# A fp32-accurate two-block kernel on one core: the places of the modulation steps, the order of the start, and four smaller orders are changed

## The reference, cut to what matters

```python
def first_block(x, c, ...):                 # D = 1024
    cond = silu(c)
    for l in range(2):
        sh1, sc1, g1, sh2, sc2, g2 = split(cond @ w_ada[l] + b_ada[l], 6)   # w_ada[l]: 1024 x 6144
        h = layer_norm(x) * (1 + sc1) + sh1
        mix = mixer(h, ...)                 # w_in, global + dilated attention, gates, w_pa, w_pb, w_out
        x = layer_norm(ALPHA * x + g1 * mix, ln1_g[l], ln1_b[l])
        h = layer_norm(x) * (1 + sc2) + sh2
        ffn = moe(h, ...)                   # router: best group of 4 experts, top 2 of 16, then gate/up/down
        x = layer_norm(ALPHA * x + g2 * ffn, ln2_g[l], ln2_b[l])
    return x

def second_block(x, mem, ...):              # two layers: h = rms_norm(x); retention, pooling, neighbourhood
    ...                                     # attention, attention to mem; gates, w_branch, w_out; then a ffn
```

## Time and profile before

| | before |
|---|---|
| time, median of 3 executions | 1797.58 us (1797.54 to 1797.79) |
| the profiled execution's own time | 1800.65 us |
| its span | 1798.80 us |
| mean granted TensorE clock | 0.976 |
| instructions | 27507 |
| the chain that ended last, by engine | PE 74%, DVE 9%, ACT 5%, POOL 5%, issue 5% |
| HBM read | 390.46 MB, 218 GB/s over the span |
| 1 MB weight transfer, issue to landing | 5.1 to 5.9 us median by name |

### The profile page before, as it was taken

The page is one execution under the profiler, slowest core; times in us unless marked ns, Lnnn a source line. Parts: engine busy times, 40 slices in busy tenths (PEclk is TensorE's granted clock), DMA queues, the critical chain, the costliest instruction groups (busy, mean ns, idle before and its releaser), DMA issues.

```text
span 1798.8 us, 27507 instructions
## 1 busy us (share of the span) xinstructions
PE 1709.0 (95%) x11564; PEld 1506.1 (84%) x11564; DVE 1171.6 (65%) x1288; ACT 939.8 (52%) x1057; POOL 224.6 (12%) x209
## 2 busy tenths in 40 slices
PE   4999997999889999799989999999999999999999
PEld 2888885888678888588869889899999989989998
DVE  2537658899864766889987475565446756665443
ACT  4435535877543554678756454354445545354442
POOL 0330010000024001001004400200001610210000
PEclk9999998999989999899989999999999999999999
DMA  9985566999848525499956445466655644546552
GB/s 363 320 275 181 176 212 235 363 373 374 289 146 282 175 101 190 181 382 376 358 178 222 120 138 165 141 211 211 207 184 184 188 130 129 188 141 209 186 186 76
DMA packets 207306, 393.28 MB, mean 219 GB/s; under 512 B 6129, under 2 KB 143345, under 8 KB 191313
## 3 DMA queue, kind: packets, MB, share of 16 engines
q1 hardware_dynamic: 204768, 381.71, 61.3%
q0 software_dynamic: 1712, 7.50, 1.2%
q10 hardware_dynamic: 704, 2.33, 0.4%
HBM read 390.46 MB, written 1.05 MB: 218 GB/s over the span
## 4 chain that ended last, share of the span: by engine, by line
PE 74%; DVE 9%; ACT 5%; POOL 5%; issue 5%; DMA 1%; SPq 0%; POOLq 0%; DVEq 0%; ACTq 0%
PE ps L546 21%; PE ps L548 21%; PE ps L547 21%; DVE low L1916 3%; PE ps L644 2%; ACT whi L1326 2%; POOL TB L2799 1%; PE ps L847 1%; PE ps L815 1%; DMA AR<-in_w_ada 1%; PE ps L830 1%; PE ps L663 1%; PE ps L564 1%; DVE small L1978 1%; POOL T L2692 1%
## 5 line engine op out<-in xcount | busy, mean ns | idle before, releaser
L1916 DVE TENSOR_TENSOR low<-raw,whi 128x2048 fp32r<-128x2048 f32 x310 | 714.6, 2315 | 393.5 <-ACT whi L1326 391.8
L1326 ACT ACTIVATE whi<-raw 128x2048 fp32r<-128x2048 f32 x310 | 591.4, 1913 | 335.3 <-PE ps L548 305.5
L546 PE MATMUL ps<-Hh,whi 128*128 128x256 f32 x1536 | 438.8, 286 | 0.0
L547 PE MATMUL ps<-Hl,whi 128*128 128x256 f32 x1536 | 434.4, 283 | 0.0
L548 PE MATMUL ps<-Hh,low 128*128 128x256 f32 x1536 | 434.4, 283 | 0.0
L546 PE MATMUL ps<-whi,Hh 128*128 128x256 f32 (+1 forms) x896 | 294.4, 329 | 27.1 <-DVE T L1964 9.9
L546 PEld LDWEIGHTS ps<-Hh,whi 128*128 128x128 f32 x1536 | 294.3, 192 | 17.4 <-issue 16.9
L547 PEld LDWEIGHTS ps<-Hl,whi 128*128 128x128 f32 x1536 | 294.4, 192 | 0.5
L548 PEld LDWEIGHTS ps<-Hh,low 128*128 128x128 f32 x1536 | 294.4, 192 | 0.0
L547 PE MATMUL ps<-low,Hh 128*128 128x256 f32 (+1 forms) x896 | 289.7, 323 | 0.0
L548 PE MATMUL ps<-whi,Hl 128*128 128x256 f32 (+1 forms) x896 | 289.4, 323 | 0.0
(11 more groups left out here) (325 smaller groups left out, 2161.5 us busy)
## 6 DMA issues: line engine op xcount, KB each, us to landing
raw<-in_w_gu SPq DMA_DIRECT2D x80, 1024.0 KB, 5.6
raw<-in_w_ff SPq DMA_DIRECT2D x66, 1024.0 KB, 5.1
raw<-in_w_in SPq DMA_DIRECT2D x58, 1024.0 KB, 5.9
raw<-in_w_d SPq DMA_DIRECT2D x40, 1024.0 KB, 5.7
raw<-in_w_gate SPq DMA_DIRECT2D x32, 1024.0 KB, 5.4
ada<-in_w_ada SPq DMA_DIRECT2D x18, 1024.0 KB, 7.1
G<-in_w_ada SPq DMA_DIRECT2D x16, 1024.0 KB, 8.4
raw<-in_w_out SPq DMA_DIRECT2D x16, 1024.0 KB, 5.0
```

Source lines behind the costliest of these rows:

```text
L546: pe.matmul(out, lhs[0], rhs[0], start=start, stop=False)
L547: pe.matmul(out, lhs[0], rhs[1], start=False, stop=False)
L1326: act.activation(wide(i, whi), wide(i, raw), ACT.Copy).then_inc(*up("w_hi", i))
L1916: dve.tensor_tensor(wide(i, low), wide(i, raw), wide(i, whi).bitcast(F32), ALU.subtract).then_inc(*up("w_lo", i))
```

## The change

It does this:

- Start: PE lifts only tile 0 ahead of steps 4 to 7 and sums 2 and 3, and tile 1 behind them; the second "qa" bank is taken when tile 1 begins. ACT makes hi 0, lift 0, hi 1 to 3, then issues the transfer of `rows`, then lift 1. DVE makes lo 0 within lift 0, then lo 1 to 3, then lift 1.
- Modulation: a new place "x1" stands between the transposes of the router's two tiles. Layer 0 takes steps 31 to 33 at x1, 34 and 35 at rt, 36 to 41 at the end of its moe ("ff"); layer 1 takes 42 at vd2, 43 at qk1, 44 to 46 at x1 and 47 at rt. Sums 15 (rt), 16 and 17 (moe) and 18 (ff) are made in layer 0, 19 (vd1), 20 (vd2), 21 (qk2), 22 (rt) and 23 (moe) in layer 1. Slots, rows and SP's order of transfers follow; two slots lie over the buffer B. ACT's turn "rt" stands right behind the sigmoid, ACT's mod_out 18 and 19 ahead of the first norm of layer 1.
- End of layer 1's moe: put_back(0) and put_back(1) stand ahead of mem_lift(0) on PE, and ACT and DVE split the unit for the last down product ahead of it.
- Second block, layer 0: DVE lifts tile 0 after tile 1's first half of the residual; PE lifts it between mk and mv of the second memory tile; ACT makes the norm of tile 1 after the copy of mv.
- ACT's copies of the turned rq and rk each stand one place sooner, in both layers.
- The second block's `out_proj` lifts tile 0 ahead of part i == 3.

```diff
@@ -214,11 @@
 MOD_PLACES = ["qa", "vd1", "vd2"] + [f"qk{i}" for i in range(6)] + [f"at{i}" for i in range(10)] + ["pa", "out", "xT", "rt"]
-MOD_TAKEN = [{"qa": (8, 9)} | {place: (10 + i,) for i, place in enumerate(MOD_PLACES[1:])},
-             {"qa": (35,)} | {place: (36 + i,) for i, place in enumerate(MOD_PLACES[1:13])}]
-MOD_SUMMED = [{"vd2": 4, "pa": 13, "xT": 14, "moe": 15} | {f"qk{i}": 5 + i // 2 for i in (1, 3, 5)} | {f"at{i}": 8 + i // 2 for i in (1, 3, 5, 7, 9)},
-              {"vd1": 16, "vd2": 17} | {f"qk{i}": 18 + i // 2 for i in (1, 3, 5)} | {f"at{i}": 21 + i // 2 for i in (1, 3, 5)}]
+MOD_TAKEN = [{"qa": (8, 9)} | {place: (10 + i,) for i, place in enumerate(MOD_PLACES[1:22])}
+             | {"x1": (31, 32, 33), "rt": (34, 35), "ff": (36, 37, 38, 39, 40, 41)},
+             {"vd2": (42,), "qk1": (43,), "x1": (44, 45, 46), "rt": (47,)}]
+MOD_SUMMED = [{"vd2": (4,), "pa": (13,), "xT": (14,), "rt": (15,), "moe": (16, 17), "ff": (18,)}
+              | {f"qk{i}": (5 + i // 2,) for i in (1, 3, 5)} | {f"at{i}": (8 + i // 2,) for i in (1, 3, 5, 7, 9)},
+              {"vd1": (19,), "vd2": (20,), "qk2": (21,), "rt": (22,), "moe": (23,)}]
@@ -238,7 @@
+start = (nc.sbuf_base + 31) // 32 * 32
 B = sb("Bh", [P, 8, S], F32R), sb("Bl", [P, 8, S], F32R)
+Bf = [nc.alloc_sbuf_tensor_at(f"Bf{i}", [P, 2048], F32, offset=start + 8192 * i) for i in range(2)]
@@ -378,14 @@
 mod_slot = [TB, G0, G1, AR0, AR1, AR[:, 4096:6144], T2, ada, TB, G0, G1, AR0]
-mod_slot += [ada, G0, G1, ada, G0, G1, ada, G0, ada, G0, ada] + [AR0, ada] * 4 + [ada]
-mod_slot += [ada, AR0, AR1, ada, AR0, ada, G0, G1, ada, G0, ada, G0, ada, G0, ada, G0]
+mod_slot += [ada, G0, G1, ada, G0, G1, ada, G0, ada, G0, ada] + [AR0, ada] * 3 + [AR0, AR1, ada, Bf[0], Bf[1], ada, Bf[0]]
+mod_slot += [ada, AR0, AR1, AR[:, 4096:6144], ada, AR0, ada, G0, ada, Bf[0], Bf[1], ada]
...
-    return AR[:, 8448:8960] if j in (1, 3) else AR[:, 7936:8448]
+    return AR[:, 8448:8960] if j in (1, 3, 16, 18, 20) else AR[:, 7936:8448]
+def mod_acc_after(j):
+    return [i for i in range(j) if (i in (1, 3, 16, 18, 20)) == (j in (1, 3, 16, 18, 20))][-1:]
@@ -489,27 @@
 load(number["A", 0, "pb"] + 7)
-for s in (29, 30):
+load_mod(sp, 29)
+sp.wait_ge(*at("mm", "pv", 0, 2, 2))
+load_mod(sp, 30)
+load_mod(sp, 31)
+load(number["A", 0, "pa", 1] + 7)
+sp.wait_ge(*at("mm", "pa", 0, 3))
+load_mod(sp, 32)
+load_mod(sp, 33)
+load(number["A", 0, "out", 3] + 7)
+for s in (34, 35, 36):
     load_mod(sp, s)
-load(number["A", 0, "out", 3] + 7)
-for s in (31, 32):
-    load_mod(sp, s)
 sp.wait_ge(*at("mm", "gather", 0, 3))
-for s in (33, 34):
+for s in (37, 38):
     load_mod(sp, s)
 load(number["A", 1, "qa", 0] + 6)
-for s in (35, 36):
+sp.wait_ge(*at("y_lo", 0, 0, 1))
+sp.wait_ge(*at("y_lo", 0, 1, 1))
+for s in (39, 40, 41, 42):
     load_mod(sp, s)
-for name, s in ((("ka",), 37), (("vd", 0), 38), (("vd", 1), 39), *((("qk", i), 40 + i) for i in range(6)),
-                (("gate", GATE_ORDER[0]), 46), (("gate", GATE_ORDER[1]), 47)):
-    load(number["A", 1, *name] + 7)
-    if s == 38:
-        sp.wait_ge(*at("x_new", 0, "ff", 1))
-    elif s == 39:
-        sp.wait_ge(*at("H_lo", ("A", 1, 1), 1, 1))
+sp.wait_ge(*at("x_new", 0, "ff", 1))
+load_mod(sp, 43)
+load(number["A", 1, "qk", 1] + 7)
+load_mod(sp, 44)
+load(number["A", 1, "pa", 1] + 7)
+sp.wait_ge(*at("mm", "pa", 1, 3))
+for s in (45, 46):
     load_mod(sp, s)
 load(number["A", 1, "out", 3] + 7)
+load_mod(sp, 47)
@@ -628,7 @@
 for i in range(4):
-    if turn_first and i == 2:
+    if turn_first and i == 3:
@@ -649,8 @@
 def mod_turn(l, place):
-    if place in MOD_SUMMED[l]:
-        mod_sums(MOD_SUMMED[l][place])
+    for j in MOD_SUMMED[l].get(place, ()):
+        mod_sums(j)
@@ -752,12 @@
 us = [unit("A", l, *x) for x in (("qa", 0), ("qa", 1), ("ka",), ("vd", 0))]
-b = [bank(pe, "qa", l, t) for t in range(2)]
+b = bank(pe, "qa", l, 0)
 bk, bv = bank(pe, "ka", l), bank(pe, "vd", l, 0)
 for t in range(2):
+    if t:
+        b = bank(pe, "qa", l, 1)
     for a in range(2):
         H_ready(sid, t, a)
-        part(us[a], a, t, b[t]).then_inc(*up("mm", "qa", l, t, a))
+        part(us[a], a, t, b).then_inc(*up("mm", "qa", l, t, a))
@@ -940,6 @@
     leave(("xT", l, t, kq), ("xT", l, t, kq))
+if t == 0:
+    mod_turn(l, "x1")
@@ -1076,17 @@
         mod_bcast(l, 5)
-if l:
-    mem_lift(0)
...
+if l:
+    mem_lift(0)
...
-    for s in (32, 33, 34):
+    for s in MOD_TAKEN[0]["ff"]:
         mod_step(s)
+    mod_sums(18)
@@ -1098,9 @@
 for n, u, b in zip(("mk", "mv"), us, bs):
+    if l and t and n == "mk":
+        lift(sid, xn, 0, "a_norm", *sid, 0)
     row_tile(u, (n, l), b, t, ("B", l, "m") if n == "mk" else None)
-if t == 0:
-    lift(sid, xn, 0, "a_norm", *sid, 0)
+    if l == 0 and t and n == "mk":
+        lift(sid, xn, 0, "a_norm", *sid, 0)
@@ -1303,12 @@
 pe.wait_ge(*at("cons_in"))
-for t in range(2):
-    lift(("A", 0, 1), xn, t, "a_norm", "A", 0, 1, t)
+lift(("A", 0, 1), xn, 0, "a_norm", "A", 0, 1, 0)
...
+lift(("A", 0, 1), xn, 1, "a_norm", "A", 0, 1, 1)
@@ -1404,8 @@
 act.wait_ge(*at("mm", "step", mod_last[j]))
-if j >= 2:
-    act.wait_ge(*at("mm", "mod", j - 1 if j > 4 else j - 2))
+for i in mod_acc_after(j):
+    act.wait_ge(*at("mm", "mod", i))
@@ -1481,6 @@
 act.activation(R[:, 0:32], R[:, 96:128], ACT.Sigmoid).then_inc(*up("scores", l))
+mod_turn(l, "rt")
@@ -1541,8 @@
 taken("A", l, "gu", n, 1)
-if n == 0:
-    mod_turn(l, "rt")
@@ -1568,26 @@
 act_hi(NT - 1)
+taken("A", l, "d", NT - 2)
 if l:
     mem_lift(0)
-taken("A", l, "d", NT - 2)
...
-    mod_out(2)
-    mod_out(3)
     hi(0)
-    hi(1)
     lift(sid, modc(0, 1), modc(0, 0), 0, ("mod_cols", 3))
-    hi(2)
+    for i in range(1, 4):
+        hi(i)
+    act.dma_start(rows[:, :], dr["rows"].partition_broadcast(P)).then_inc(*up("rows_in", by=16))
     lift(sid, modc(0, 1), modc(0, 0), 1)
-    hi(3)
 else:
     taken("A", 0, "d", NT - 1)
+    for j in (18, 19):
+        mod_out(j)
     ln(sid, 0)
-    mod_out(16)
+    mod_out(20)
@@ -1615,7 @@
 if i == 0:
-    act.wait_ge(*at("mm", "step", 36 if l else 11))
+    act.wait_ge(*at("mm", "step", 41 if l else 11))
@@ -1747,19 @@
     taken("B", 0, "d", 8)
+else:
+    taken("A", 1, "d", NT - 1)
...
-else:
-    taken("A", 1, "d", NT - 1)
-rms((*sid, 1), x[:, 1, :], xn[:, 1, :], xn[:, 1, :], small(3, 1), *ready[1])
+    rms((*sid, 1), x[:, 1, :], xn[:, 1, :], xn[:, 1, :], small(3, 1), *ready[1])
...
+if l == 0:
+    rms((*sid, 1), x[:, 1, :], xn[:, 1, :], xn[:, 1, :], small(3, 1), *ready[1])
@@ -1774,11 @@
 taken("B", l, "nq")
+leave_bank(tile["rqT"], ("T", "rq", l), "T_a", "rq", l)
 square("nk", l, (("mm", "nk", l), ps("nk", l)), ("head_d", "nq", l))
 taken("B", l, "nk")
-leave_bank(tile["rqT"], ("T", "rq", l), "T_a", "rq", l)
+leave_bank(tile["rkT"], ("T", "rk", l), "T_a", "rk", l)
 taken("B", l, "nv")
-leave_bank(tile["rkT"], ("T", "rk", l), "T_a", "rk", l)
@@ -1896,7 @@
 ln_act(("A", 0, 1, 1), 1, "x_in")
-act.dma_start(rows[:, :], dr["rows"].partition_broadcast(P)).then_inc(*up("rows_in", by=16))
+mod_out(2)
+mod_out(3)
@@ -1963,6 @@
 ins.then_inc(*up("lift_d", sid, t, 0))
+between()
@@ -2025,6 @@
 lift(sid, scale, bias, 0, *ready)
+mod_turn(0, "ff")
@@ -2293,12 @@
     mod_fin(j)
-lo(0)
-lift(sid, modc(0, 1), modc(0, 0), 0, "mod_cols", 3)
-lo(1)
+lift(sid, modc(0, 1), modc(0, 0), 0, "mod_cols", 3, between=lambda: lo(0))
+for i in range(1, 4):
+    lo(i)
 lift(sid, modc(0, 1), modc(0, 0), 1, "mod_cols", 3)
-lo(2)
-lo(3)
@@ -2449,10 @@
 half, whole = residual(*after)
-for t in range(2):
-    half(t, 0)
-    half(t, 1)
-    whole(t)
+half(0, 0)
+half(0, 1)
+whole(0)
+taken("A", 1, "d", NT - 1)
+half(1, 0)
+lift(("B", 0, 1), col("mix_g", 0, 8), None, 0)
+half(1, 1)
+taken("B", 0, "mk")
+whole(1)
@@ -2473,10 @@
 sid = "B", l, 1
-if l == 0:
-    taken("A", 1, "d", NT - 1)
-lift(sid, col("mix_g", 8 * l, 8), None, 0)
-taken("B", l, "mk")
+if l:
+    lift(sid, col("mix_g", 8 * l, 8), None, 0)
+    taken("B", l, "mk")
```

More of the change, by code:

```diff
@@ L1935, in mod_turn @@
             def mod_turn(l, place):
-                if place in MOD_SUMMED[l]:
-                    mod_fin(MOD_SUMMED[l][place])
+                for j in MOD_SUMMED[l].get(place, ()):
+                    mod_fin(j)
             def ln_factors(sid, t):
@@ L1950, in ln_factors, with lift @@
                                          ).then_inc(*up("ln_bias", *sid, t))
-            def lift(sid, scale, bias, t, *ready):
+            def lift(sid, scale, bias, t, *ready, between=lambda: None):
                 out = turned_rows(sid)
```

## The result

| | before | changed |
|---|---|---|
| time, median of 4 executions | 1797.68 us (1797.54 to 1798.06) | 1778.70 us (1778.45 to 1780.56) |
| span of the profiled execution | 1798.80 | 1776.9 |
| mean granted clock | 0.976 | 0.982 |

The ratio of the times is 0.9896, with a 95% interval of 0.9879 to 0.9913: 19.0 us faster, where 29.3 was forecast. 1778.7 lies inside the range of 1760 to 1781, near its upper end, and above the likeliest case of 1764 to 1773. A second timing of the changed kernel on another chip gave 1777.09 against 1797.66 (0.9882, 0.9866 to 0.9899).

A forecast was written before the change was run, and what follows sets the result against it. PE, busy 95% of the span, bounds the kernel, so time is won in its waits and open work; memory is at its limit only at the start. Terms summed to −29.3, giving 1768.3 us from the median 1797.58; range 1760 to 1781.

The forecast's parts named there:

- part 7: End of layer 1 and second block's start: put_back first gives −2.4, the earlier lift of tile 0 gives −5.7.
- the attention: Layer 1's attention loses steps and sums: −2.9, ends −6 and −1; nothing counted at at0 and at1.
- layer 0's router: Steps fill PE's wait, but mod_outs, a sum and two steps delay what follows: +1.0, ends +3.5 and −2.9.
- the end of layer 0: Six steps and sum 18 instead of three steps; late loads delay layer 1's dense start: +1.4, ends 0 and +3.5.
- Start: First weight matmul at 37.7 instead of 45.41, as tile 1's lift moves behind the steps: −8.0, ends −9.5 and 0.
- Rival (b): Memory bounds the start, so its 8.0 is lost: 1776.3, up to 1782; chance 0.22 together with Rival (e).
- Projections: Layer 1's projections, qa to qk5: 2 steps and 3 sums instead of 9 and 5, −9.5, ends −11 and −8.
- Layer 1's router: Three steps in the gap cost nothing and some clock returns: −0.8, ends −3.1 and +1.0.
- First expert: Layer 0's first expert: moving ACT's turn rt ahead removes PE's wait and the low clock behind it: −3.4, ends −2.0 and −4.0.
- Rival (e): put_back ahead of the memory's lift fails if splits block it; part 7 worth 1, 1775; chance 0.22 together with Rival (b).
- rqT, rkT: PE's two waits of 1.6 for ACT's copies go: −3.1, ends −3.1 and −1.
- Rival (a): Steps in the routers' gaps and at layer 1's start keep the clock at 2.4 GHz: 1760.7; chance 0.15.

The follow-up runs named there:

- u_start: Changed kernel with the start of before on all engines and both qa banks taken first; 1784.97 us, 0.9936 of the kernel before.
- u_rt: Changed kernel with ACT's turn rt back in the expert loop at n == 0; first-expert stage 18.20 us instead of 14.52.
- ctrl: The kernel before, unchanged, profiled once more; span 1796.9 us.
- after2: The changed kernel once more, on another chip; 1777.09 us, span 1775.3.
- rt_cols: Changed kernel with steps 34 and 35 streaming 128 of 512 columns; logits' last product to placing product 3.53 us, against 5.63 in after2.
- u_pb: Changed kernel with the memory's lift ahead of put_back(0) again; end of layer 1 54.01 us instead of 50.39 to 50.56.
- rt_short: Changed kernel with steps 34 and 35 making one of four column blocks; logits' last product to placing product stayed at 6.17 us.
- best: Changed kernel with step 41 at vd2, 42 at at0, 43 at at1, sum 18 at vd1, 20 at qk1, out_proj's lift at i == 2; 1766.94 us, 0.9825 of before.

## Why the prediction was right in sign and 10 us too far

The forecast of 1768.3 was 10.4 below the measured 1778.7. The two profiled executions differ by 21.9, and 3 us of that is no property of the change: the first profile of before stood 3.07 above its median, the changed kernel's at its median. The points below are read in this pair, where −21.9 stands against −29.3, and the last paragraph on the stages, below, shows where those 3 us lie. Beside the tile's order in part 7, three terms came out beyond the ends that they had been given: the attention (+0.4, the end was −1), layer 0's router (+3.9, +3.5) and the end of layer 0 (+4.4, +3.5).

1. **Start**, −8.0: −7.9 measured, and shown by u_start. Rival (b) did not occur, although the share rose to 1.07. One reading in it is wrong without effect: the row at 28.13, x16, is steps 4 and 5 alone; 6 and 7 follow it until 33.65.
2. **Projections**, −9.5: from layer 1's first matmul to the first product of the attention (588.18 before, 572.90 after) it was −9.9.
3. **Attention**, −2.9: +0.4 from there to the router. This is the step that failed most plainly: "at0 and at1 I count nothing". Right about the wait, which came as said (3.31 for DVE's copies), wrong about what it does to the clock: 0.50 over 6.8 us behind it. u_rt, without the low stretch, has the 2.7 back. Another 0.9 is a wait that the sum did not have: with the step ahead of the attention gone, PE waits 0.85 for ACT's copy (L841 <- ACT L1413) where it had not waited. The extra sums cost 0.9 in layer 0's experts and 0.5 at layer 1's, within the +1.8.
4. **Layer 0's router**, +1.0: +3.9 (ctrl to after2: +4.3). I priced a step at the full clock's 0.99, but in the low stretch a step takes 1.94 and a sum 1.85, so the sum and two steps ahead of the placing product took 5.3 where a step and a wait of 1.08 had stood. Before, and then changed:

```profile
285.33 1.94 PE L644 MATMUL ps<-ada,cpad 128*32 128x512 f32 x8
288.35 1.00 PE L967 MATMUL ps<-TB,ones 128*128 128x12 f32 x4 [1.08 <-DVE TB L2096]
...
275.18 1.85 PE L687 MATMUL ps<-ones,AR 128*128 128x1 f32 x8
276.95 1.93 PE L668 MATMUL ps<-ada,cpad 128*32 128x512 f32 x8
278.66 1.94 PE L668 MATMUL ps<-Bf,cpad 128*32 128x512 f32 x8
280.52 1.03 PE L995 MATMUL ps<-TB,ones 128*128 128x12 f32 x4
```

rt_cols shows 2.1 of it. Another 1.0 lies between tile 1's transposes (11.03 ahead of before) and the logits (10.06); ACT's two mod_outs stand there ahead of the hi, as had been said, but no run took them away. The last 0.6 is the gather, 6.39 instead of 5.76, more of which lies in the low clock. **Layer 1's router**, −0.8: about 0 up to the gather, +0.7 from there, the gather taking 6.53 instead of 5.71. Steps and a sum filled the waits there (4.96 and 2.95 became 2.24 and 0.63), but the clock was low for 10.2 us still, 13.7 before and in after2.
5. **First expert**, −3.4: −3.6, shown by u_rt.
6. **End of layer 0**, +1.4: +4.4 (114.65 to 119.06 from the middle of the experts, both with a low stretch near 450). The landing was right: 41's step began at 486.6 + 9.8 (what the changed kernel is ahead by there) = 496.4 on the time of before, where 495.9 had been said. Left out was sum 18, which stands between that step and the lift and takes 1.87 in the low clock; and the cover was misread: the residual does not free PE at a time of its own but follows the lift by 6.3. By the estimate from the Trainium skill ("DMA: Bandwidth & Descriptors", section "Anatomy of one DMA — SWDGE (gpsimd) path") the term would have been +0.3. That fit is of GpSimd's path, and these loads are SP's: in the changed kernel those of steps 40 and 41 took 6.3 and 8.8, and step 42's, alone on the queue, 5.1, not 4.4. So the rows were the better guide, and neither held the sum.
7. **End of layer 1, second block's start**, −8.1: −7.2, in other shares: put_back 3.5 instead of 2.4, since its waits had also let the clock fall (its products go from 0.63 to 0.39), and the tile's order 2.7 instead of 5.7, outside the 3.5 to 6.5 that was given, since the lift of tile 1 waits 2.2 for its norm, which had been named as late next but priced at nothing. Rival (e) did not happen: u_pb gives the 3.5.
8. **rqT, rkT**, −3.1: −2.8. 9. **out_proj**, +2.3: +1.8.

From 122 to 262 us the changed kernel is another 3.9 shorter, which no step foresaw (139.30 to 135.44; ctrl, without the low stretch at 250, took 138.33). The changed kernel shows neither low stretch, and the two are what the 3.9 consists of: 2.3 around the one at 233, 1.6 around the one at 250. Neither is shown to be a gain of the change. At the first, PE waits just ahead for a step (0.67, in ctrl 1.32), and rt_short, whose kernel is the changed one up to its router, has that wait (1.58, at 225.83) and a low stretch too. The step in before and in the changed kernel:

```profile
232.88 1.52 PE L644 MATMUL ps<-ada,cpad 128*32 128x512 f32 x8 [0.67 <-DMA ada<-in_w_ada]
...
224.97 1.07 PE L668 MATMUL ps<-ada,cpad 128*32 128x512 f32 x8
```

The stage from the first weight matmul to layer 0's router takes 216.02 in rt_short, 216.38 and 216.19 in the two executions of before, and 212.2 to 213.2 in the nine other profiles that start from the changed kernel and have no low stretch there; u_pb and best, with one like that at 250, take 215.0. Why PE waits there in both profiles of before and in one of the other twelve, and whether the change makes that rarer, is open. Without these 3.9 the two profiles differ by 18.0, and the medians by 19.0.

Rival (a) did not happen. The mean clock rose from 0.976 to 0.982, but in layer 0's router it stayed at 0.50 from 271.4 to 288.5, longer than before:

```profile
271.40:288.50 17.10, 14.90 (x75) 10.58 (x76) 10.84 (x38) 4.04 (x7) 0.00 (x0) 0.50 0.35 117
```

PE is busy for 14.9 of these 17.1 us, 3.6 of them with two steps of w_ada. So the steps did not keep the clock up there. In the Trainium skill ("TensorE: Matmul & The Clock Gate", "Part 1: The HAM clock gate") activity releases the clock; here busy time alone did not, and which activity would, these runs don't tell.

## What to carry to other kernels

A hole of PE that the sum puts at nothing, because another engine ends the stage anyway, can still have a price: the products behind it may run at half clock. Fill such holes with the independent work that is at hand (in the attention two steps kept the clock, in the routers the steps did not), and price what stands in them at the clock that the window shows there, not at the one where the row was read. And before a stretch is called covered, ask whether the cover starts by itself or follows the work that is being delayed.

## What the runs showed of the hardware

- Four matmuls of 128x32 held and 512 streamed, each into its own 32 rows of PSUM, take as long as one: 1.93 for x8 and 1.91 for x2, both at clock 0.50 (1.06 for x8 at 1.00). Cut to 128 columns, the eight take 0.65 at clock 0.50.
- Low-clock stretches lasted 3.4 to 20.5 us, and the same kernel has them at partly other places from one execution to the next: of the two profiles of the changed kernel one has a stretch at 445 and the other one at 676. One stretch cost 1.6 to 2.7, or 2.3 to 3.1 with the wait ahead of it, and the executions of one kernel lie up to 6.6 us apart (best: 1763.89 at a mean clock of 0.988, 1770.50 at 0.984). That is as much as most of the single edits here, so those were read from distances between products and not from times.
- A matmul's row and its weight load's row can name different releasers for one wait; at the bank that ACT frees (u_rt, 299.79) the weight load's was the right one.
